# A two-layer decoder on one core: the recurrence's end inside the output stage, and the norm and the first queries by token tile

## The reference, cut to what matters

```
for l in (0, 1):
    h = rmsnorm(x, norm_mix[l])
    if l == 0:                           # gated linear recurrence
        xb, yb, qm = split(h @ a_w_in)   # 768, 768, 256
        xb = causal_conv(xb)
        a, u = gates(xb)                 # decay and input for each token and channel
        state[t] = a[t] * state[t-1] + u[t]
        mix = state * gelu(yb)
    else:                                # three-branch attention on shared keys and values
        mix = nsa_attention(...)
    mo = memory_attention(qm, mem)
    x = x + concat(mix, mo) @ w_out[l]                  # 1024 x 1024
    x = x + peer(rmsnorm(x, norm_ffn[l]), peer_wq[l], subkeys, u, v)
```

## Time and profile before

| | us |
|---|---|
| median of three runs | 3248.51 (3245.14 to 3250.86) |
| the profiled execution's own time | 3254.94 |
| its span, first to last instruction | 3252.9 |
| PE busy | 3190.3 (98%) |
| VectorE busy | 2015.2 (62%) |
| GpSimd busy | 1900.8 (58%) |
| ScalarE busy | 1237.9 (38%) |

### The profile page before, as it was taken

One profiled execution on the slowest core, in us unless ns is written; L12 is line 12 of the kernel. 1 busy time (PEld: TensorE's weight loads), 2 busy tenths in 40 slices (PEclk: granted clock), 3 DMA queues, 4 the chain that ended last, 5 costly groups with the idle time before them and its releaser, 6 DMA issues. The chain is left out here.

```text
span 3252.9 us, 47592 instructions
## 1 busy us (share of the span) xinstructions
PE 3190.3 (98%) x15034; PEld 2600.2 (80%) x15034; DVE 2015.2 (62%) x4044; ACT 1237.9 (38%) x1835; POOL 1900.8 (58%) x1315
## 2 busy tenths in 40 slices
PE   8989999999999999999899999999999999999999
PEld 7678888888888788887767778888888887878887
DVE  5756675752224888888646765757632225888888
ACT  3633333334343333333426743333332223333333
POOL 0006888888888655555000008888888886555554
PEclk9999999999999999999998999999999999999999
DMA  5925665566668999999318215656566668999998
GB/s 189 344 86 133 133 136 118 134 149 142 147 144 243 352 355 348 351 354 337 127 35 293 92 63 120 147 118 148 124 146 145 145 145 287 354 347 347 356 353 296
DMA packets 399380, 681.94 MB, mean 210 GB/s; under 512 B 145472, under 2 KB 239680, under 8 KB 399040
## 3 DMA queue, kind: packets, MB, share of 16 engines
q1 hardware_dynamic: 218944, 520.95, 47.2%
q0 software_dynamic: 155648, 134.82, 20.6%
q10 hardware_dynamic: 24704, 25.17, 2.3%
HBM read 560.85 MB, written 119.94 MB: 209 GB/s over the span
## 5 line engine op out<-in xcount | busy, mean ns | idle before, releaser
L1770 POOL DMA_INDIRECT gate_matrix<-pe_misc x768 | 1284.9, 1673 | 871.6 <-DVE pe_misc L2341 638.0
L2039 PE MATMUL psum<-split,ex_ah 128*128 128x512 f32 x2976 | 921.9, 391 | 11.7 <-DVE ex_al L2484 11.4
L431 PE MATMUL psum<-up_hhi,up_hi 128*128 128x512 f32 x2048 | 798.1, 390 | 0.0
L431 PE MATMUL psum<-up_hlo,up_hi 128*128 128x512 f32 x2048 | 796.8, 389 | 0.0
L431 PE MATMUL psum<-up_hhi,up_lo 128*128 128x512 f32 x2048 | 796.8, 389 | 0.0
L422 DVE TENSOR_TENSOR up_lo<-up_raw,up_hi 128x1024 fp32r<-128x1024 f32 x256 | 313.9, 1227 | 758.8 <-ACT up_hi L418 750.5
L2039 PEld LDWEIGHTS psum<-split,ex_ah 128*128 128x128 f32 x2976 | 556.4, 188 | 139.4 <-DVE ex_al L2484 22.5
L2039 PE MATMUL psum<-split,ex_al 128*128 128x512 f32 x1488 | 579.7, 390 | 0.0
L1780 POOL DMA_INDIRECT ex_gv<-in_v,ga_at x256 | 273.5, 1068 | 336.0 <-DVE x_sb L2434 316.5
L431 PEld LDWEIGHTS psum<-up_hhi,up_lo 128*128 128x128 f32 x2048 | 384.5, 188 | 79.7
L431 PEld LDWEIGHTS psum<-up_hhi,up_hi 128*128 128x128 f32 x2048 | 384.6, 188 | 79.2
(11 more groups left out here) (372 smaller groups left out, 3153.0 us busy)
## 6 DMA issues: line engine op xcount, KB each, us to landing
up_raw<-in_uT SPq DMA_DIRECT2D x256, 512.0 KB, 3.7
ro_wq<-in_v SPq DMA_DIRECT2D x256, 512.0 KB, 5.5
gelu<-up_z SPq DMA_DIRECT2D x256, 256.0 KB, 2.2
pe_misc<-gelu SPq DMA_DIRECT2D x256, 192.0 KB, 5.6
ex_gm<-gate_matrix SPq DMA_DIRECT2D x124, 384.0 KB, 5.8
gate_matrix<-ga_at ACTq DMA_DIRECT2D x8, 3072.0 KB, 18.2
gate_matrix<-ga_at SPq DMA_DIRECT2D x8, 3072.0 KB, 23.3
ro_wq<-in_peer_wq SPq DMA_DIRECT2D x32, 512.0 KB, 4.6
```

The source lines that it names most:

```text
L431: last = pe.matmul(self.ps[:, a, :], w[:, a, dc, :], h[:, dc, :], start=(dc == 0 and m == 0), stop=(dc == DC - 1 and m == 2))
L1770: pool.indirect_dma_start(place, bass.IndirectOffsetOnAxis(ap=to[:, j:j + 1], axis=0), gates[:, j:j + 1], None, compute_op=ALU.add).then_i ...
L2039: last = pe.matmul(psy[:, o, :], w[:, par, a, toks], v[:, par, a, cols], start=False, stop=(final and m == 2))
```

## The change

- `front0` no longer does scans 3 to 5, the six products with the gelu, or the last gelu. `y` lives on into the next stage. The rows of `w_out` for the two memory channels are loaded beside the first two rows, by two transfers in place of one.
- `out_norm` of layer 0 starts with the two memory channels (they lie in PSUM, and the products need their banks), then does what was left of the recurrence between its splits. The chunks of `w_out` are taken in that order.
- In both layers the norm's weights are copied once into a row that is read without stride, the addition of a tile is one instruction of 1024 elements instead of two of 512, the transposes of tile 1 and 2 go to other PSUM banks (`TURNED`), and the lists of VectorE and ScalarE are reordered.
- `first_queries` handles one token tile of 128 columns instead of half of the tokens. `out_norm` does tiles 0 to 2, `peer` does tile 3.

```diff
         if n == 10:
             sp.wait_ge(s["kv"].sem, s["kv"].done(3))
-            sp.dma_start(wo[:], k.dram["w_out0"][0:4 * P, :].rearrange("(c p) d -> p c d", p=P)).then_inc(s["wo"].sem, 16)
-    sp.wait_ge(s["wo"].sem, s["wo"].base + 16)
+            for at, block_ in ((0, LRU_CH), (MEM_CH, 0)):
+                sp.dma_start(wo[:, at:at + 2, :], k.dram["w_out0"][block_ * P:(block_ + 2) * P, :].rearrange(
+                    "(c p) d -> p c d", p=P)).then_inc(s["wo"].sem, 16)
+    sp.wait_ge(s["wo"].sem, s["wo"].base + 32)
...
     act.activation(whi[:, 0, :], wo[:, 0, :], ACT.Copy).then_inc(s["split"].sem, 1)
     act.drain()
     for i in range(NL - 1):
         gelu(i)
     step(13)
-    act.drain()
-    gelu(NL - 1)
...
     dve.tensor_tensor(wlo[:, 0, :], wo[:, 0, :], whi[:, 0, :].bitcast(F32), ALU.subtract)
-    for i in range(3, NL):
-        scan(i)
-    dve.drain()
-    for i in range(NL):
-        dve.wait_ge(s["gelu"].sem, s["gelu"].done(i))
-        dve.tensor_tensor(tnh[:, i, :], tnh[:, i, :], y[:, i, :], ALU.mult)
...
-def first_queries(pe, k, up, wqh, wql, b, half, between=None):
-    toks = slice(half * S // 2, (half + 1) * S // 2)
+def first_queries(pe, k, up, wqh, wql, b, t):
+    toks = slice(t * P, (t + 1) * P)
     for dc in range(DC):
-if between is not None and dc == 3:
-    between()
...
+TURNED = (0, 4, 0, 6)
 def turned(t):
-    return ps[:, 2 * t:2 * t + 2, :].rearrange("p h (c e) -> p (h c) e", e=P)
+    return ps[:, TURNED[t]:TURNED[t] + 2, :].rearrange("p h (c e) -> p (h c) e", e=P)
...
         for o in (0, 1, 4, 5, 6, 7, 2, 3):
             if mix and dc == 0 and o == 2:
-                pe.wait_ge(s["mixlo"].sem, s["mixlo"].done(first.index(DC - 1)))
+                pe.wait_ge(s["mixlo"].sem, s["mixlo"].done(MEM_CH - 1))
             last = products(dc, o, False)
         last.then_inc(s["prod"].sem, 1)
     pe.wait_ge(s["wlo"].sem, s["wlo"].done(DC - 1 - ready))
+    if mix:
+        pe.wait_ge(s["mixlo"].sem, s["mixlo"].done(DC - 1))
     for t in range(TT):
         if t == TT - 1:
             turn(0)
         for h in range(2):
             for dc in (DC - 2, DC - 1):
                 last = products(dc, 2 * t + h, dc == DC - 1)
-            if t == TT - 1 and h == 0:
-                turn(1)
         last.then_inc(s["prod"].sem, 1)
-    pe.wait_ge(s["lo"].sem, s["lo"].done(1))
+    turn(1)
+    pe.wait_ge(s["lo"].sem, s["lo"].done(0))
     for b in range(2):
         pe.wait_ge(wq_lo.sem, wq_lo.done(b))
-        first_queries(pe, k, up, wqh, wql, b, 0, None if b == 0 else lambda: turn(3))
-        if b == 0:
-            turn(2)
+        first_queries(pe, k, up, wqh, wql, b, 0)
+    pe.wait_ge(s["lo"].sem, s["lo"].done(1))
+    first_queries(pe, k, up, wqh, wql, 0, 1)
+    turn(2)
+    first_queries(pe, k, up, wqh, wql, 1, 1)
+    turn(3)
+    pe.wait_ge(s["lo"].sem, s["lo"].done(2))
+    for b in range(2):
+        first_queries(pe, k, up, wqh, wql, b, 2)
...
+    def mix_high(dc):
+        if dc >= MEM_CH:
+            act.wait_ge(s["mixed"].sem, s["mixed"].done(dc - MEM_CH))
         act.activation(up.hhi[:, dc, :], mix[dc], ACT.Copy).then_inc(s["mixhi"].sem, 1)
-        if dc == 1:
-            high(1)
-    for dc in rest:
+    if mix:
+        mix_high(0)
+        mix_high(1)
+        high(1)
+        act.activation(rec.gate[:, LRU_CH - 1, :], rec.gate[:, LRU_CH - 1, :], ACT.Gelu_apprx_tanh).then_inc(s["gelu"].sem, 1)
+        mix_high(2)
+        mix_high(3)
+        high(2)
+        mix_high(4)
+        mix_high(5)
+        high(3)
+        mix_high(6)
+        mix_high(7)
+    for dc in rest[2:] if mix else rest:
         high(dc)
     for b in range(2):
         act.wait_ge(peer_.wq_loaded[b].sem, peer_.wq_loaded[b].base + 16)
         act.activation(wqh[:, b, :, :], peer_.wq[:, b, :, :], ACT.Copy).then_inc(wq_hi.sem, 1)
     act.activation(dump[:, 0:1], k.col("rowvalid"), ACT.Sqrt)
     act.drain()
-    for t in range(TT):
-        square(t)
-        root(t)
-        if t >= 1:
-            h_high(t - 1)
-    h_high(TT - 1)
+    square(0)
+    root(0)
+    square(1)
+    root(1)
+    h_high(0)
+    square(2)
+    root(2)
+    h_high(1)
+    square(3)
+    root(3)
+    h_high(2)
+    h_high(3)
...
     def add(t):
         dve.wait_ge(s["prod"].sem, s["prod"].done(DC - 2 + t))
-        for h in range(2):
-            part = x[:, t, h * 512:(h + 1) * 512]
-            last = dve.tensor_tensor(part, part, ps[:, 2 * t + h, :], ALU.add)
-        last.then_inc(s["added"].sem, 1)
+        dve.tensor_tensor(x[:, t, :], x[:, t, :], ps[:, 2 * t:2 * t + 2, :].rearrange("p h m -> p (h m)"),
+                          ALU.add).then_inc(s["added"].sem, 1)
...
-        dve.scalar_tensor_tensor(out=xn[t].rearrange("p (c e) -> p c e", c=DC), in0=x[:, t, :].rearrange("p (c e) -> p c e", c=DC),
-                                 scalar=rstd[:, t:t + 1], in1=row.rearrange("p (e c) -> p c e", c=DC),
+        dve.scalar_tensor_tensor(out=xn[t], in0=x[:, t, :], scalar=rstd[:, t:t + 1], in1=weights,
                                  op0=ALU.mult, op1=ALU.mult).then_inc(s["xn"].sem, 1)
...
+    def mix_low(dc):
+        dve.wait_ge(s["mixhi"].sem, s["mixhi"].done(dc))
         dve.tensor_tensor(up.hlo[:, dc, :], mix[dc], up.hhi[:, dc, :].bitcast(F32), ALU.subtract).then_inc(s["mixlo"].sem, 1)
-        if dc == 1:
-            low(1)
-    for dc in rest:
+    def scan(i):
+        dve.tensor_tensor_scan(rec.state[:, i, :], rec.decay[:, i, :], rec.given[:, i, :], 0.0, ALU.mult, ALU.add)
+    def gated(i):
+        if i == LRU_CH - 1:
+            dve.wait_ge(s["gelu"].sem, s["gelu"].done(0))
+        dve.tensor_tensor(rec.state[:, i, :], rec.state[:, i, :], rec.gate[:, i, :], ALU.mult).then_inc(s["mixed"].sem, 1)
+    if mix:
+        mix_low(0)
+        mix_low(1)
+        low(1)
+        for i in range(3):
+            gated(i)
+        scan(3)
+        mix_low(2)
+        scan(4)
+        mix_low(3)
+        low(2)
+        scan(5)
+        dve.drain()
+        for i in range(3, LRU_CH):
+            gated(i)
+        mix_low(4)
+        low(3)
+        mix_low(5)
+        mix_low(6)
+        mix_low(7)
+    for dc in rest[2:] if mix else rest:
         low(dc)
     for b in range(2):
         dve.wait_ge(wq_hi.sem, wq_hi.done(b))
         dve.tensor_tensor(wql[:, b, :, :], peer_.wq[:, b, :, :], wqh[:, b, :, :].bitcast(F32),
                           ALU.subtract).then_inc(wq_lo.sem, 1)
+    dve.wait_ge(s["row"].sem, s["row"].base + 16)
+    dve.tensor_copy(weights.rearrange("p (c e) -> p c e", c=DC), row.rearrange("p (e c) -> p c e", c=DC))
+    dve.drain()
     add(0)
     mean_square(0)
+    scale(0)
     add(1)
-    dve.wait_ge(s["row"].sem, s["row"].base + 16)
-    scale(0)
+    add(2)
     mean_square(1)
-    add(2)
     scale(1)
+    h_low(0)
     mean_square(2)
-    h_low(0)
+    add(3)
     h_low(1)
-    add(3)
     scale(2)
     mean_square(3)
     scale(3)
...
-        first_queries(pe, k, up, wqh, wql, b, 1).then_inc(queried.sem, 1)
+        first_queries(pe, k, up, wqh, wql, b, TT - 1).then_inc(queried.sem, 1)
...
-    mix = [k.words[:, (LRU_CH + i) * S:(LRU_CH + i + 1) * S] for i in range(LRU_CH)] + [k.psum[:, 2 + r, :] for r in range(MEM_CH)]
+    y = k.sb(c, "f0_y", [P, LRU_CH, S])
+    front0(k, x, up, pe.wq, pe.misc, ga, rope, wo, kv, last, gmat, rows, y)
+    early = k.words[:, 0:2 * LRU_CH * S].rearrange("p (a n t) -> p a n t", a=2, n=LRU_CH)
+    rec = Recurrence(early[:, 0, :, :], last[:].rearrange("p (a n t) -> p a n t", a=2, n=DC)[:, 1, :, :], early[:, 1, :, :], y)
+    mix = [k.psum[:, 2 + r, :] for r in range(MEM_CH)] + [rec.state[:, i, :] for i in range(LRU_CH)]
     wo2 = last[:, 0:4 * D].rearrange("p (c d) -> p c d", c=4)
-    out_norm(k, 0, x, up, pe, wo[:], wo2, last[:, 4 * D:6 * D], rows, 1, mix)
+    out_norm(k, 0, x, up, pe, wo[:], wo2, [last[:, n * D:(n + 1) * D] for n in (4, 5, 7)], rows, 1, mix, rec)
```

More of the change, by code:

```diff
@@ L496, in softplus_of, with front0 @@
     dve.drain()
-def front0(k, x, up, wq, misc, ga, rope, wo, kv, last, gmat, rows):
+Recurrence = namedtuple("Recurrence", "decay given state gate")
+def front0(k, x, up, wq, misc, ga, rope, wo, kv, last, gmat, rows, y):
     nc = k.nc
@@ L521, in front0 @@
         "ksq": 2, "kmean": 1, "keps": 1, "kroot": 1, "kr": 1, "kb": 1, "kn": 1,
-        "exps": 2, "left": 2, "rooted": 2, "gelu": NL, "split": 1, "rows": 16 * LAYERS,
+        "exps": 2, "left": 2, "rooted": 2, "split": 1, "rows": 16 * LAYERS,
         "scored": A, "maxed": A, "expd": A, "scaled": A, "turn": 2 * A, "stored": 2 * A, "summed": A})
@@ L905, in gelu @@
             def gelu(i):
-                act.activation(y[:, i, :], y[:, i, :], ACT.Gelu_apprx_tanh).then_inc(s["gelu"].sem, 1)
-            act.wait_ge(s["wo"].sem, s["wo"].base + 16)
+                act.activation(y[:, i, :], y[:, i, :], ACT.Gelu_apprx_tanh)
+            act.wait_ge(s["wo"].sem, s["wo"].base + 32)
```

(33 more changed lines are left out.)

9 lines of the change are left out of this document (3 added, 6 removed).

## The result

| | before | after |
|---|---|---|
| median us, 20 runs each | 3248.88 (3244.57 to 3251.65) | 3252.43 (3247.74 to 3260.36) |
| ratio, 95% interval | | 1.0016 [1.001, 1.0021] |
| profiled execution's own time | 3254.94 | 3249.42 |
| its span | 3252.9 | 3247.3 |

What follows compares the result with a forecast made beforehand. PE was taken as the bound, busy 98% of the span, with gains up to its first score matmul passing one for one. -9.5 + 4.45 + 4.45 = -0.6 us gave a median of 3248, range 3231 to 3257.

Steps and rivals of the forecast that it cites:

- the gap: PE's idle time ahead of layer 0's first output product, forecast to shrink from 10.05 to 3.0 us.
- the copy: Norm weight row copied once on VectorE, inside its 3.5 us wait before the first addition: nothing lost, 2.1 us at most.
- s: Start of the first addition in each layer's norm, 205.80 and 1899.66 us before; the queries were forecast at s+10.15.
- B: Rival: no floor for narrow query matmuls, cost by columns, 0.067 us each; total change -17.5 us, 3231; 20%.
- D: Rival: load and stream of narrow query matmuls don't overlap fully, 0.14 us each; total change +11 us, 3259.5; 8%.
- The 64-column row: Trace row of 128x128 weights with 64 moving columns, 0.110 us each, read as a floor set by weight load.
- part 3: Queries by token tile, both layers: 192 matmuls at 0.110, 21.1 us, 9.5 us more PE work per layer.
- Parts 2 and 3: Norm chain and narrow queries: the norm hands PE back 3.3 us per layer; with the queries each layer loses 4.45.
- C: Rival: the clock falls in the 3.0 us gap before layer 0's output products; total change +1.9 us, 3250.4; 13%.
- part 1: Recurrence's end moved into layer 0's output stage: 7.05 us earlier start plus 2.48 from the clock, 9.5 us gained.
- the clock stays: Layer 0's output products keep full clock because the 3.0 us gap is shorter than 5 us; worth 2.48 us.

Runs made afterwards that it cites:

- norm_only: The kernel before with the new norm, single additions and 128-column queries, the recurrence left where it was; 3263.14 us, ratio 1.0047.
- half_queries: The kernel after with queries in halves of 256 columns again, the rest of the norm new; 3234.28 us, ratio 0.9955.
- part1_only: The kernel before with only the recurrence's end moved, norm and 256-column queries unchanged; 3240.39 us, ratio 0.9977.
- boundary_filled: The kernel after with unread wide matmuls on both sides of the stage change amid the narrow queries, both layers; 3260.59 us, ratio 1.0036.
- gap_filled: The kernel after with twelve unread 512-column matmuls at the end of the first stage; 3254.02 us, ratio 1.0014.
- half_filled: The kernel after with 256-column queries and twelve unread 512-column matmuls at the end of the first stage; 3237.13 us, ratio 0.9962.

## Why the prediction was wrong

Right, with their numbers: the end of the first stage and the gap (2.99 for 3.0; product at 159.68, 0.9 earlier than said, since PE's work of the first stage ended that much earlier in this execution); no stall by what was moved; the copy hidden; addition 1.22, scaling 1.28; queries from s+9.9 (said 10.15); the spacing of a 128-column matmul, 0.111 for 0.110, so rivals B and D fell; the longer way from addition to score, +4.3 in each layer for +4.45. The 81 ns of the Trainium skill (TensorE: Matmul & The Clock Gate, Back-to-back issue gap), weighed under B, don't hold for these weights: the traces have 0.111 us. The 64-column row was the right one to read the floor from.

Wrong: the clock, at two places. **The step that failed is the schedule of part 3**, "192 x 0.110 = 21.1 us" and "Nothing waits any more", which prices every narrow matmul at full clock. The prediction itself put a stage change of 0.8 us in the middle of them and took it for 0.8 us. In four of five profiles the clock fell there, which cost 2.6 to 4.7 us more up to the first score and 1.5 behind it: 4.1 to 6.2 us, or 4.3 on the mean of the five (an estimate from these profiles). Parts 2 and 3 came to +14.3 us (norm_only, medians) instead of +8.9. half_queries, without the narrow matmuls, has neither the added work nor this fall. No rival held that: C looked for the clock in the 3.0 us gap alone, and D, the slower one, put the loss in the spacing at full clock.

The smaller miss is the 2.48 us of part 1, "the clock stays": in the 3.0 us gap, or within about 1 us behind it, it fell in seven of the nine profiles that have this gap, as rival C says, and product to addition then took 37.3 to 38.6 us instead of 35.65. In part1_only and boundary_filled it stayed, and took 35.7. So the premise that 3.0 us is short enough, since the fall before came after 5 us, was wrong. The mean over the nine is 1.7 us lost. Part 1 as a whole gave 8.5 us (part1_only) instead of 9.5; gap_filled, part1_only and boundary_filled show that the fall, not the splits, sets that time.

With both, the two kernels that each hold one part add up to -8.5 + 14.3 = +5.8, and the predicted sum with the two falls as estimated from the profiles gives -0.6 + 4.3 + 1.7 = +5.4. Measured is +3.6 by the medians, +5 (3 to 7) by the ratio. The profiled execution of after is shorter than that of before (span -5.6) because neither is typical: after had no fall at the stage change, and before lost more than usual elsewhere. From layer 0's first score, 235.49 and 231.03, the lead of 4.5 us grew to 9.8 at layer 1's first product, in code that the change doesn't touch, where the clock dips at other places in each execution: summed over stretches of 10 us, the share of the clock that was missing comes to 29.0 us in the profile of before and 13.8 in that of after, and between those two points to 20.4 and 10.2. That these dips make the 5.4 us is likely, but no run tested it. Comparing the two profiles alone would have given the wrong sign.

What stays open: why part of the executions escape the fall with the same code, at the stage change and in the 3.0 us gap alike; why 64-column matmuls lose the clock without any gap; and whether gap_filled and half_filled kept the clock by their filler or by chance, as two of nine kept it without.

## What to carry to other kernels

Cutting a product into narrower pieces so that it can start earlier pays only down to the width at which the weights set the pace; here 128 columns cost 0.111 us and 256 cost 0.121, and waiting 2.5 us for the wider piece won by 7.3 us in layer 0. Don't let a run of such narrow matmuls span a stage change, and reckon with half clock if you do. A wait of 2.4 us ahead of wide ones can cost a fall too, 1.5 us in half_filled. A norm chain shortened on its engines (plain weight row, one addition, new order) was worth 3 us per layer once the queries stayed wide: half_queries, 3234.3, is the version to keep.

## What the hardware did that I had not expected

- PE busy without a gap on 64-column matmuls fell to 0.50 some 5 us after they began, and stayed there for 78 us in layer 0 (at 128 columns it was 1.00 over 45 us). At half clock a narrow matmul takes 0.208 to 0.214 us.
- After PE's gap of 0.75 us at the stage change, half clock came in five of six profiles where it lay among 128-column matmuls, and lasted about until they and the scores ended. Among 256-column ones gaps of 0.75 to 1.3 us in the same place brought it in none of four.
- 128 moving columns cost 0.111 us on 128x128 weights and 0.06 us on weights of 64 columns, in a row that differs in other things too.
- With a gap filled by unread work the clock stayed, but the work held the stage's end, 1.6 us for the 1.6 that it gave back.
